# A decoder-trunk kernel: latent rows computed in one piece per tile, expert rows and outputs stored from GpSimd's queue

## The reference, cut to what matters

```python
for layer in range(DEPTH):                       # DEPTH = 2
    if layer % 2 == 0: yp, buf_p, _ = _even_mixer(xp, None, 0, *ew)      # pooling | gating
    else:              yp, S_p, sh_p, c_p, k_p = _odd_mixer(xp, ...)     # RWKV-7 | latent attention
    xp = _layernorm(ALPHA * xp + yp, ln_g[layer, 0], ln_b[layer, 0])
    xp = _layernorm(ALPHA * xp + _moe(xp, ...), ln_g[layer, 1], ln_b[layer, 1])
...
def _odd_mixer(x, ...):
    p = x @ w_in                                 # 1024 -> 2208 columns
    ... _rwkv7(p[..., :C_COLS], ...)             # first 1792 columns
    ... _mla_project(p[..., C_COLS:], ...)       # last 416 columns: the latent rows
...
def _moe(x, ...):                                # 16 experts, best group of 4, then top 2
    for e in range(N_EXPERTS):
        he = jax.nn.silu(h @ w_gate[e]) * (h @ w_up[e])
        y = y + gates[:, e:e + 1] * (he @ w_down[e])
```

## Time and profile before

| | |
|---|---|
| median of 3 runs | 1244.89 us (1242.97 to 1245.06) |
| the profiled execution, its own time | 1242.97 us |
| its span in the profile | 1241.1 us |
| mean granted clock of PE | 0.947 of full speed |
| PE busy | 1109.3 us (89%) |
| DVE, ACT, POOL busy | 508.0, 306.8, 93.5 us |
| HBM read, written | 205.63 MB, 58.16 MB |

### The profile page before, as it was taken

How to read it: one execution, slowest core, us unless ns; L and a number is a source line. 1 busy time by engine, 2 the same in 40 slices (tenths; PEclk the granted TensorE clock), 3 DMA queues, 4 the chain that set the end, 5 groups by cost and what they waited for, 6 DMA issues and landing times.

```text
span 1241.1 us, 19108 instructions
## 1 busy us (share of the span) xinstructions
PE 1109.3 (89%) x7210; PEld 673.9 (54%) x7210; DVE 508.0 (41%) x1322; ACT 306.8 (25%) x703; POOL 93.5 (8%) x115
## 2 busy tenths in 40 slices
PE   7999994699999379999899998999999749999985
PEld 3686442344444146677688876555555324444431
DVE  2570336011111383479635555665433621111117
ACT  0102113111111131413244332354511321111112
POOL 0010002000000300000121111210000120000011
PEclk9999996799999779999999998999999869999997
DMA  9568008899993533122322242845510589999634
GB/s 354 208 240 171 1 1 331 337 341 367 371 375 147 199 133 143 35 83 76 92 76 70 75 134 78 303 144 213 212 68 1 224 344 354 363 362 372 234 125 179
DMA packets 85380, 246.28 MB, mean 198 GB/s; under 512 B 9488, under 2 KB 50496, under 8 KB 66720
## 3 DMA queue, kind: packets, MB, share of 16 engines
q1 hardware_dynamic: 64304, 153.15, 33.9%
q0 software_dynamic: 11760, 58.24, 13.3%
q10 hardware_dynamic: 9216, 33.56, 7.5%
HBM read 205.63 MB, written 58.16 MB: 213 GB/s over the span
## 4 chain that ended last, share of the span: by engine, by line
PE 85%; DVE 6%; DMA 4%; issue 3%; POOL 1%; ACT 1%; POOLq 0%; SPq 0%; DVEq 0%; ACTq 0%
PE bank L1214 18%; PE bank L1150 11%; PE bank L1234 9%; PE bank L1384 9%; PE bank L1302 5%; PE bank L1481 4%; PE bank L1320 3%; PE bank L1356 3%; PE bank L1204 2%; PE bank L1734 1%; PE bank L1759 1%; PE bank L1164 1%; DMA work<-yrows,rowi 1%; PE bank L1141 1%; PE bank L1461 1%
## 5 line engine op out<-in xcount | busy, mean ns | idle before, releaser
L1150 PE MATMUL bank<-ring,cat 128*128 128x512 f32 (+1 forms) x320 | 141.0, 594 | 1.3 <-ACT cat L1914 1.3
L1214 PE MATMUL bank<-ring,work 128*128 128x512 f32 x256 | 114.2, 598 | 0.0
L1384 PE MATMUL bank<-xT,ring 128*128 128x288 f32 x448 | 110.9, 407 | 0.0
L2322 DVE TENSOR_TENSOR work<-work,bank 128x256 f32<-128x256 f32 x32 | 13.5, 421 | 219.1 <-ACT work L1884 219.1
L1384 PEld LDWEIGHTS bank<-xT,ring 128*128 128x128 f32 x448 | 84.6, 190 | 24.1 <-issue 1.5
L1150 PEld LDWEIGHTS bank<-ring,cat 128*128 128x128 f32 (+1 forms) x320 | 56.0, 179 | 74.0 <-issue 73.9
L1214 PEld LDWEIGHTS bank<-ring,work 128*128 128x128 f32 x256 | 48.2, 193 | 54.3 <-issue 54.3
L1884 ACT ACTIVATE work<-bank 128x256 f32<-128x256 f32 x32 | 12.3, 385 | 207.9 <-PE bank L1214 207.9
L1302 PE MATMUL bank<-xT,ring 128*128 128x288 f32 x256 | 63.1, 407 | 0.0
L1204 PE MATMUL bank<-const,work 128*128 128x128 f32 x256 | 36.4, 292 | 29.3 <-DMA work<-xrows 29.3
L1234 PE MATMUL bank<-ring,work 128*128 128x512 f32 x128 | 57.7, 593 | 1.0 <-issue 1.0
(11 more groups left out here) (434 smaller groups left out, 1846.1 us busy)
## 6 DMA issues: line engine op xcount, KB each, us to landing
ring<-in_stream_dram SPq DMA_DIRECT2D x71, 1024.0 KB, 7.1
cat<-in_stream_dram SPq DMA_DIRECT2D x16, 1024.0 KB, 9.0
work<-xrows ACTq DMA_DIRECT2D x32, 512.0 KB, 5.5
xT<-in_stream_dram SPq DMA_DIRECT2D x16, 1024.0 KB, 8.0
work<-in_stream_dram SPq DMA_DIRECT2D x16, 1024.0 KB, 9.5
yrows<-work ACTq DMA_DIRECT2D x32, 512.0 KB, 6.0
by_batch<-in_pages_dram SPq DMA_DIRECT2D x128, 128.0 KB, 2.3
xrows<-work POOLq DMA_DIRECT2D x1, 8192.0 KB, 27.7
```

What stands on the lines that cost most here:

```text
L1150: i = pe.matmul(bank(n)[0:ROWS[tile], :], cat[:, k, tok(tile)], slot(w[k // 4], 4, 512)[:, k % 4, :], start=(k == 0), stop=(k == KC - 1))
L1214: i = pe.matmul(bank(n), xgT[:, e % 2, k, :], sparse_slot(layer, 3 * e + k // 4, 4, 512)[:, k % 4, :], start=(k == 0), stop=(k == KC - 1))
L1384: i = pe.matmul(bank(n + s)[:, 0:nn], slot(w, KC, 256)[:, k, P * (m % 2):P * (m % 2) + P], xT[:, k, a:a + nn], start=(k == 0), stop=(k == ...
```

## The change

Four edits. The latent rows of a tile become one piece of 16 matmul instructions that waits for both weight blocks and both halves of x at its start; it stands on PE behind the turn of the next tile, and the jobs are numbered in that order. The stores of the experts' rows leave ACT and are issued by POOL, each when both halves of the expert are in `yS`, ahead of the gathers. The five stores of the output x leave SP and are issued by POOL behind the last mixture, and POOL's wait for its stores takes them in. The semaphore `combined` becomes one per layer.

```diff
             reserve(f"xT{tile}", 2)
-            reserve(f"dtok{tile}")
+            if tile > 0:
+                reserve(f"dtok{tile - 1}")
+        reserve(f"dtok{NT - 1}")
...
-        combined = sem("combined")
-        x_stored = sem("x_stored")
+        combined = [sem(f"combined{k}") for k in range(LAYERS)]
...
-            for tile in range(NT):
-                sp.wait_ge(ln_done, (2 * LAYERS - 1) * NT + tile + 1)
-                sp.dma_start(outs["x"][:, D_MODEL * tile:D_MODEL * tile + D_MODEL], x[:, tile, :]).then_inc(x_stored, 16)
-            sp.wait_ge(x_stored, 16 * NT)
...
                 with pool.Else():
+                    for e in range(N_EXP):
+                        landed(pool, ejob(layer, e, "D0"), 2)
+                        pool.dma_start(yrows[P * e:P * e + P, :], yS[:, e % NYS, :]).then_inc(y_stored[layer][e % NYS], 16)
                     for i in range(NYS):
...
             pool_mixture(1)
+            for tile in range(NT):
+                pool.wait_ge(ln_done, (2 * LAYERS - 1) * NT + tile + 1)
+                store(pool, outs["x"][:, D_MODEL * tile:D_MODEL * tile + D_MODEL], x[:, tile, :])
             pool.wait_ge(stored, 16 * n_stores[0])
...
-                def latent_rows(tile, q):
-                    if (tile, q) in ((0, 0), (0, 1)):
-                        w.append(weights(pe, ("oin", 7 + q)))
+                def latent_rows(tile):
+                    w = [weights(pe, ("oin", 7 + q)) for q in range(2)]
                     n = job(f"dtok{tile}")
-                    landed(pe, job(f"xT{tile}", q), 1)
-                    if q == 0:
-                        claim(pe, n)
-                    for k in range(4 * q, 4 * q + 4):
+                    landed(pe, job(f"xT{tile}"), 2)
+                    claim(pe, n)
+                    for k in range(KC):
...
                 for tile in range(NT):
                     turn_x(f"xT{tile}", 1, tile)
                     if tile > 0:
-                        latent_rows(tile - 1, 1)
-                    latent_rows(tile, 0)
-                latent_rows(NT - 1, 1)
+                        latent_rows(tile - 1)
+                latent_rows(NT - 1)
...
-                            if e > 1:
-                                store_rows(e - 2)
...
-                            if e == N_EXP:
-                                store_rows(N_EXP - 2)
...
-                    store_rows(N_EXP - 1)
...
-                    dve.sem_inc(combined, 2 * NT)
...
-                                                 acc[0:r, tile, :], ALU.mult, ALU.add).then_inc(combined, 1)
-                        dve.wait_ge(combined, 2 * NT * layer + 2 * tile + k + 1)
+                                                 acc[0:r, tile, :], ALU.mult, ALU.add).then_inc(combined[layer], 1)
+                        dve.wait_ge(combined[layer], 2 * tile + k + 1)
```

More of the change, by code:

```diff
@@ L1345, in odd @@
             def odd():
-                w = []
-                def latent_rows(tile, q):
-                    if (tile, q) in ((0, 0), (0, 1)):
-                        w.append(weights(pe, ("oin", 7 + q)))
+                def latent_rows(tile):
+                    w = [weights(pe, ("oin", 7 + q)) for q in range(2)]
                     n = job(f"dtok{tile}")
-                    landed(pe, job(f"xT{tile}", q), 1)
-                    if q == 0:
-                        claim(pe, n)
-                    for k in range(4 * q, 4 * q + 4):
+                    landed(pe, job(f"xT{tile}"), 2)
+                    claim(pe, n)
+                    for k in range(KC):
                         i = pe.matmul(bank(n)[0:ROWS[tile], 0:D_COLS], xT[:, k, tok(tile)],
-                                      slot(w[q], 4, 512)[:, k % 4, 0:D_COLS], start=(k == 0), stop=(k == KC - 1))
-                    if q == 1:
-                        done(i, n)
+                                      slot(w[k // 4], 4, 512)[:, k % 4, 0:D_COLS], start=(k == 0), stop=(k == KC - 1))
+                    done(i, n)
                 for tile in range(NT):
@@ L1854, in load_rows @@
                         act.dma_start(xg[:, e % NXG, :], xrows[P * e:P * e + P, :]).then_inc(xg_loaded[layer][e % NXG], 16)
-                    def store_rows(e):
-                        landed(act, ejob(layer, e, "D0"), 2)
-                        act.dma_start(yrows[P * e:P * e + P, :], yS[:, e % NYS, :]).then_inc(y_stored[layer][e % NYS], 16)
                     act.wait_ge(scattered[layer], 32 * NT)
```

## The result

| | before | after |
|---|---|---|
| median | 1243.93 us (4 runs, 1242.39 to 1245.06) | 1255.49 us (4 runs, 1251.92 to 1259.28) |
| ratio | | 1.0097, 95% interval 1.0073 to 1.012 |
| the profiled execution, its own time; its span | 1242.97; 1241.1 us | 1256.15; 1254.3 us |
| mean granted clock of PE | 0.947 | 0.943 |
| PE busy | 1109.3 us | 1112.7 us |

The kernel is slower by 1243.93 x 0.0097 = 12.1 us (9.1 to 14.9). The forecast was 3.5 us, and the range ended at 1250.8.

A forecast was written before the change was run, and what follows sets the result against it. PE, busy 1109.3 of 1241.1 us, was taken as the bound. The terms 1.5 + 1.2 + 0.85 = 3.55 us on the median 1244.89 gave 1248.4 us; own range 1246.6 to 1250.6, 8-in-10 range 1244.8 to 1250.8.

The forecast's parts named there:

- The output stores: +0.85 us.: At the kernel's end, POOL's last x store reacts and lands 0.75 us later than SP's, plus 0.1 us wake-up.
- rival 3: At both handovers and the end, POOL's stores as slow as its 1024 KB one: 8.8 us, 1253.7; chance 0.06.
- The last expert store: +0.75 us, twice.: At each layer's mixture end, POOL reacts 0.2 us later than ACT and its store lands 0.55 us later.
- Rival 1: At both handovers and the end, POOL's stores land as fast as ACT's and SP's: 1.9 us, 1246.8; chance 0.22.
- The latent rows: +1.2 us.: At the odd layer's start, PE waits for the second weight block, then runs 16 matmuls partly at lower clock: +1.2 us.
- Rival 4: At the odd layer's start, PE is warm and the latent rows gain 1.1 us: 1.25 us in all, 1246.1; chance 0.08.
- The steady part: nothing.: Inside the mixtures, moving 15 of 16 expert stores per layer costs nothing, since PE is busy throughout.
- rival 2: At the odd layer's start and recurrence, clock changes win back up to 3.4 us: 0.15 us, 1245.0; chance 0.14.

The follow-up runs named there:

- only_y_on_pool: The kernel before with only the stores to yrows (the experts' stores) issued by POOL ahead of the gathers: 1245.54 us, ratio 1.0000 (0.9983 to 1.0018).
- after_x_on_sp: The kernel after with the five stores of the output x back on SP: 1246.34 us, ratio 1.0019 (1.0002 to 1.0036) to the kernel before.
- first_x_on_pool: The kernel before with the x store of tile 0 alone on POOL, tiles 1 to 4 on SP: 1242.86 us, ratio 0.9987 (0.9975 to 0.9999).

## Why the prediction was wrong, point by point

**The failed step is "The output stores: +0.85 us."** It measured 9.2 us by position (12.2 instead of 3.0 from DVE's last pass to the end; by the times, with 82 DMAs of POOL's instead of 114, the stores alone cost 7.7). The step's own two items held: POOL issued 0.29 us behind DVE, as forecast, and the store landed in 2.9 us, 0.3 sooner than forecast. What it left out is what POOL does behind its last wait. The step ended the program 0.5 us behind the landing, on the model of POOL's wake-up; the profile has the drain of 8.65 us there. The row was in the trace of before, 16.9 us long at 1206.5, but hidden and in no view of busy time, and the argument looked only at work that counts as busy. The rivals didn't have it either: rival 3 reached 8.8 us, but by slow landings at three places, which the 2.9 us refute.

**The last expert store: +0.75 us, twice.** Layer 0 lost 0.74 and layer 1 0.46, so 1.2 instead of 1.5. The items differ: the reaction was 0.5 us instead of 0.29, the landing 2.9 instead of 3.2 (the estimate by the Trainium skill's page DMA: Bandwidth & Descriptors, quoted there, was 3.2 too, 0.3 above the row), and layer 1 got 0.25 back at POOL's wake-up. Rival 1 (the same landing) is refuted by a small margin. What came on top, about 1.3 us at the 32 matmuls behind the gathers, is a clock cost that the step did not count.

**The latent rows: +1.2 us.** Measured +1.2 at the start of the odd phase, in the mean of the profiles; that the mean gives just the forecast is in part luck. Against before's own profile, from which the step was worked out, the kernel after shows -0.35 from the first gather on and +1.2 from the second block's issue on. And the step let all that follows move along by its 1.2 us, where at layer 1's copy only 0.2 are left in three of four profiles. Turn 1 went inside the wait, the 16 matmuls took 7.97 us (forecast 7.9) and the odd phase began 478.14 - 453.14 = 25.0 us later (forecast 25.2), with no wait at turn 4. The second wait was 0.36 us instead of 1.5, since the second block came some 1.5 us sooner behind the first gather; tile 1's ln_done (442.80) stands 23.0 us behind it, as before (23.3). Rival 4 is refuted: the clock was low.

**The steady part: nothing.** PE is busy 81.94 of 82 us as before, and the stores' slower landing, 9.2 us in the median, fits into the three experts' time that the step gave it. No run has the semaphore per layer alone.

**The recurrence's clock (rival 2)** did not decide. A swing of its kind is there, 2.6 us between stretches at 0.50 of different length, but also among kernels whose edits touch nothing ahead of the last mixture: from the odd phase to the last copy of layer 1 they scatter from 722.7 to 726.3 us with and 722.5 to 725.1 without the experts' stores on POOL. In the pair of before and after nothing swung (722.5 and 723.1 us).

The forecast's own range does not quite follow from its terms: 2.05 and 4.9 us on 1244.89 are 1246.9 and 1249.8, not 1246.6 and 1250.6, and with a microsecond either way 1245.9 and 1250.8. Nothing hangs on it here.

The account by places: 9.2 + 0.74 + 0.46 + 1.3 and 0.2 to 1.2 for the latent rows, 11.9 to 12.9 us, against 12.1 (9.1 to 14.9) by the times. What stays open is why the drain costs 0.07 us for each DMA; how it behaves for few DMAs was not run, and neither was a program in which POOL issues none. The positions give the experts' stores 2.5 us, which is just outside the -2.1 to +2.2 of the times of only_y_on_pool, so that share is the least certain.

## What to carry to other kernels

Before moving the last work of a kernel to another engine, read what each engine does from its last instruction to the end of the span, not only its busy time: the row of the program's end shows whether its drain is short and whether it is hidden. On GpSimd, an output store that ended early was free and the same stores as the kernel's last act were not; if they must be there, let another engine wait for their landing, which saved 2.5 us here by position. What a small shift on the path costs is also a matter of how long PE stays at the lower clock behind it: the last handover, half a microsecond longer, went with 1.3 us more behind it, and the latent rows' 1.2 us were mostly given back. One pair of profiles does not show such a thing; several of each do.

## What the runs showed of the hardware

- GpSimd's drain at the end of its program: 6.03 us with 77 DMAs issued in the program, 8.65 us with 114, 0.07 to 0.08 us for each more, for 16 bytes as for 512 KB, and also for DMAs issued 0.8 ms earlier; SP's is 7 ns. It starts at the last issue, and its length runs beside the landing. With gathers still going out it ended 8.3 to 8.9 us behind the last gather's issue with 77 DMAs (before: 1215.04, where that issue ends, to 1223.4), and 9.7 to 10.5 us with 109 (9.7 in after_x_on_sp).
- A 512 KB store with little else in flight (an output store, or a layer's last expert store) lands in 2.9 us from POOL, in 2.6 from SP, in 2.62 from ACT. The median of the 32 experts' stores, most of them beside dense weight loads, is 9.2 to 9.5 us from POOL and 5.5 to 6.3 from ACT.
- POOL needs 0.3 us (behind one wait, output stores) to 0.5 us (experts' stores) from DVE's end to the issue, ACT 0.07.
- PE's first matmuls behind an idle time had the clock at 0.50 for 3.6 us in one profile and for 5.2 us in another, with idle times only 0.7 us apart (6.72 and 7.42 us).
- The recurrence, untouched by the edit, had 9.9 us of PE work at 0.50 in two stretches in one profile (before) and 15.4 us in another (first_x_on_pool), and the way from the odd phase to layer 1's copy took 722.5 and 725.1 us.
